# A two-block transformer kernel on one core: bias reads moved to SP's queue, GpSimd's work reordered and enlarged, convolution taps dealt anew

## The chip, the cores and the metric

The kernel runs on one core of one Trainium2 chip. The metric is the device time of one execution in microseconds. Engines are named as in the profile: PE (TensorE), DVE (VectorE), ACT (ScalarE), POOL (GpSimd), SP (SyncE, which here only issues transfers).

## The reference, cut to what matters

Two blocks run over one sequence of 256 tokens with 1024 channels, all in float32. Every large product is a projection `h @ W`.

```python
def first_block(x, ...):
    h = rms_norm(x, attn_norm_w)
    q, k, v, u, g = split(h @ w_in)                  # 1024 x (1024+1024+1024+2048+2048)
    q, k = rms_norm per head (8 heads, 2 x 64)
    p = softmax(q1 k1 * scale + bias) - lam * softmax(q2 k2 * scale + bias)   # bias from T5 buckets
    y_a = (rms_norm(p @ v) * c) @ w_proj_attn
    c = causal_depthwise_conv(u_a * sigmoid(u_b), width 31)
    y_b = silu(layer_norm(c)) @ w_proj_conv          # mean and variance over the channels
    x = x + (g_a * y_a + g_b * y_b) @ w_out
    return x + (silu(gt) * up) @ w_down              # feed-forward, 2816 wide

def second_block(x, ...):
    q, k, v, xl, gl = split(rms_norm(x) @ w_in_2)
    a = stick_breaking_attention(q, k, v)            # log-sigmoids and suffix sums
    l = rg_lru(conv4(xl)) * gelu(gl)                 # a linear recurrence over the tokens
    x = x + concat(a, l) @ w_out_2
    return x + square(relu(rms_norm(x) @ w_up)) @ w_down   # 4096 wide
```

## The kernel before

**Units.** All projections are cut into 120 units. A unit is a slab of weights of 4 x 128 rows by 512 columns (1 MB). For each unit SP issues the load into one of three `raw` slots; ACT rounds it to `w_hi` (`split_high`, L605); DVE or POOL subtracts to get the rest, `w_lo` (`split_low` L944, or L588 on POOL where `on_pool(u)` holds: units 7 to 27 without 18); PE then multiplies 4 x 2 x 3 times (L1691 to L1693: hi·hi, lo·hi, hi·lo). `w_hi` and `w_lo` have three slots too. Each engine has one program in a fixed order, a loop over the step `s`; in step `s` PE multiplies unit `s`, and ACT, DVE and POOL prepare unit `s + 2` and do the small work of that step. A load into a slot waits for the subtraction of the unit three before it (L427).

**Small work of PE.** It comes either in the middle of a unit (`halfway(s)`, after the second of four slabs) or behind it (`after(s)`). PE's small products go to four banks of `aux`; a bank is handed over by `claim`, which waits for the last reader.

**First mixer, steps 2 to 35.** The convolution is 248 taps on DVE (31 taps times 8 channel tiles of 128, L984 and L988), accumulated in `aux` bank 1, and dealt over the steps by a table:

```python
TAPS_AT = {3: 8, 4: 6, 5: 7, 6: 12, 7: 14, 8: 12, 9: 9, ..., 25: 10, 26: 12}
```

Steps 3 to 26 hold them all; `conv_last` is 26, and `LN` is 27. Taps of a pair of channel tiles need `glu_t` of that pair (`turn_glu(i)` on PE at L1504, kept by ACT at L671). A head's attention takes four steps from `HEADS[hd]` (8, 10, 12, 14, 18, 20, 22, 24): PE's scores; DVE adds the bias (L1130) and takes the maximum (L1136); ACT exponentiates; DVE makes the factor `st_mix` (L1109); POOL scales and adds the two maps (L556, L560) in step `HEADS[hd] + 2`; PE turns the result (`turn_probs`, after step `HEADS[hd] + 2`) and multiplies by v. POOL also sums conv tiles (L548, in the steps `ADDED`), scales attention outputs (L534 to L541, in the steps of `A_GROUPS`: 19, 26, 28) and raises to the power -1/2 (L484) for the norms of q and k.

**Bias.** `rel_row` is written to a scratch tensor in DRAM by POOL's queue (L514) and read back shifted by eight transfers of 128 KB, two in each of the steps 4 to 7, issued by POOL in `bias_reads` (L503 to L511). The first use is DVE's L1130 of head 0, in step 9.

**Channel norm.** When the last taps are done (step 26), DVE adds the last two conv tiles to `conv_sum` (L1220), PE makes the mean (`channel_sum(conv_sum, 0)`, halfway through step 27, in bank 2), DVE subtracts it (L1258), and squares, variance and gates follow.

**Second mixer, from step B = 74.** In the steps 80 to 85 DVE runs the recurrence (L1301 to L1313) and the softplus sums (`softplus_sum`, L1016 and L1020) which PE needs for `suffixes(n)` (L1442 to L1446): `suffixes(0)` halfway through unit 83, `suffixes(1)` behind it. ACT rounds units 83, 84 and 85 in the steps 81, 82 and 83; POOL does nothing there but the norm of q and k.

Of the kernel before, what the change touches and what calls it, by code (L numbers as in the profile page):

```python
# [14 lines left out]
P = 128  # L15
D = 1024
S = 256
# [66 lines left out]
def build(nc, a, out):  # L84
# [21 lines left out]
    PIECED = 3  # L106

# [10 lines left out]
    def on_pool(u):  # L118
        return 7 <= u <= 27 and u != 18
# [14 lines left out]
    TAPS_AT = {3: 8, 4: 6, 5: 7, 6: 12, 7: 14, 8: 12, 9: 9, 10: 15, 11: 10, 12: 12, 13: 7, 14: 12, 15: 11, 16: 4, 17: 11, 18: 16, 19: 8, 20: 12, 21: 11, 22: 12, 23: 10, 24: 12, 25: 10, 26: 12}  # L134
# [16 lines left out]
    with ExitStack() as ctx:  # L151
# [250 lines left out]
        def _(sp):  # L402
# [17 lines left out]
            for u, (c, k0, nk, _, _) in enumerate(units):  # L420
# [45 lines left out]
        def _(pool):  # L466
# [36 lines left out]
            def bias_reads(s):  # L503
                step = P // SHIFTS
                for r in range(2 * s - 8, 2 * s - 6) if 4 <= s <= step // 2 + 3 else ():
                    if r == 0:
                        pool.wait_ge(rel_stored, 16)
                    pool.wait_ge(unit_done, s)
                    src = bass.AP(tensor=rel_dram, offset=P - 1 - r,
                                  ap=[[RELS - step, SHIFTS], [RELS * SHIFTS, H], [1, S]])  # L510
                    pool.dma_start(bias[r:P:step, :, :], src).then_inc(bias_loaded, 16)  # L511

# [4 lines left out]
            for s in range(NU):  # L517
                if s < K0:
                    bias_reads(s)
                if s in ended:  # L520
# [3 lines left out]
                    if kind == "res" and i % 2 == 1 and i < 7:  # L524
                        st = stage_of(kind, i)
                        power(rstd[:, st, :], ms[:, st, :], mean_sq, st + 1, rstd_ready)
                        if st == 2:
                            qk_epsilon(2)
                for j, (at_, n0, n1) in enumerate(A_GROUPS):
# [20 lines left out]
                for hd in range(H):  # L550
                    if s == HEADS[hd] + 2:
                        pool.wait_ge(summed, 2 * hd + 2)
                        for qb in range(2):
                            n = 2 * hd + qb
                            p_1 = probs[:, 1, OFF[qb]:OFF[qb] + P * (qb + 1)]
                            nc.gpsimd.tensor_scalar(p_1, p_1, st_mix[:, n:n + 1], 0.0, ALU.mult, ALU.add)\  # L556
                                .then_inc(scaled, 1)
                        pool.wait_ge(scaled, 2 * hd + 2)
                        p_0, p_1 = probs[:, 0, 0:KEYS], probs[:, 1, 0:KEYS]
                        nc.gpsimd.tensor_tensor(p_0, p_0, p_1, ALU.add).then_inc(mixed, 1)  # L560
# [29 lines left out]
                if s >= K0:  # L590
                    bias_reads(s)
# [5 lines left out]
        def _(act):  # L597
# [109 lines left out]
            for s in range(NU + 1):  # L707
# [35 lines left out]
                if (0 < s < EARLY or s >= B) and s not in LATE and s not in (Q0, K0, LN + 2, LN + 3) and s not in NORMS and s + LEAD < NU:  # L743
# [172 lines left out]
                if s == B + 8:  # L916
                    softplus_parts(0)
                    split_high(s + LEAD)
                if s == B + 9:
                    keep_turned2(gelu_t, 0, g2_turned, g2_in)  # L920
                    softplus_parts(1)
                    split_high(s + LEAD)
                    act.wait_ge(lru_out, 1)
                    nc.scalar.activation(y_hi[:, CT2:KT, :], lru_tmp[:, :, :], ACT.Copy).then_inc(lru_hi, 1)
                    weights2(0)
# [14 lines left out]
        def _(dve):  # L940
# [124 lines left out]
            for s in range(NU + 1):  # L1065
# [691 lines left out]
```

## Time and profile before

| | |
|---|---|
| time, 3 runs | 737.78, 739.63, 741.29 us, median 739.63 |
| profiled execution | 738.59 us, of it 736.8 us from the first to the last instruction |
| PE busy | 726.5 us (99%), granted clock 1.00 |
| PE weight loads | 596.2 us (81%) |
| DVE, ACT, POOL busy | 486.3, 397.3, 167.9 us |
| HBM | 129.61 MB read, 178 GB/s over the span |

The profile is of one execution; times in it run from the first instruction. Busy PE time includes overlap of one product with the next, so the places to look at are those where PE stood idle before an instruction.

### The profile page before, as it was taken

How to read it: one execution, taken by the hardware profiler on the slowest of the kernel's cores; microseconds unless marked ns; L12 is line 12 of the kernel's file. 1: busy time of each engine (PE TensorE's matmuls, PEld its weight loads, DVE VectorE, ACT ScalarE, POOL GpSimd, SP SyncE). 2: the span in 40 equal slices, each digit the busy share in tenths (PEclk: the TensorE clock that was granted, in tenths of full speed). 3: DMA queues.
4: the chain of work that ended last, by engine and by line, in shares of the span. 5: the costliest groups of instructions: out<-in, count | busy, mean ns of one | idle time of the engine just before them, and what ended most of it. 6: DMA issues, size and time to landing. Idle time of an engine off the chain costs nothing.

```text
span 736.8 us, 9065 instructions
## 1 busy us (share of the span) xinstructions
PE 726.5 (99%) x3439; PEld 596.2 (81%) x3439; DVE 486.3 (66%) x659; ACT 397.3 (54%) x513; POOL 167.9 (23%) x118
## 2 busy tenths in 40 slices
PE   9998999999999999999999999999999999999998
PEld 7786778788788888888888888888788888888886
DVE  5598998999887665555556355668866565653531
ACT  6744667564794455444444345479846554444330
POOL 1089898998300011000000000140001000000000
PEclk9999999999999999999999999999999999999999
DMA  8866536555347546655664564642364556556540
GB/s 293 254 199 198 172 117 199 194 174 175 115 172 286 172 155 215 194 178 172 191 216 148 188 208 147 229 170 59 114 201 149 196 166 203 171 173 204 194 143 29
DMA packets 82851, 131.45 MB, mean 178 GB/s; under 512 B 4036, under 2 KB 35852, under 8 KB 82808
## 3 DMA queue, kind: packets, MB, share of 16 engines
q1 hardware_dynamic: 82272, 129.61, 53.8%
q0 software_dynamic: 528, 1.25, 0.6%
q8 instruction: 28, 0.46, 0.3%
q14 instruction: 15, 0.12, 0.0%
q10 hardware_dynamic: 8, 0.02, 0.0%
HBM read 129.61 MB, written 1.25 MB: 178 GB/s over the span
## 4 chain that ended last, share of the span: by engine, by line
PE 77%; DVE 9%; ACT 4%; POOL 4%; DMA 3%; issue 2%; SPq 0%; ACTq 0%; DVEq 0%; POOLq 0%
PE acc L1691 23%; PE acc L1693 23%; PE acc L1692 23%; PE aux L1351 4%; DVE aux L988 3%; POOL w_lo L588 3%; DMA raw<-w_in_dram 1%; ACT w_hi L605 1%; DVE w_lo L944 1%; DMA x_in<-x_dram 1%; DMA bias<-rel_scratch 1%; POOL probs L556 1%; DVE qk_ss L1151 0%; DVE w_lo L949 0%; PE aux L1397 0%
## 5 line engine op out<-in xcount | busy, mean ns | idle before, releaser
L944 DVE TENSOR_TENSOR w_lo<-raw,w_hi 128x2048 fp32r<-128x2048 f32 (+1 forms) x97 | 220.2, 2272 | 126.5 <-ACT w_hi L605 126.5
L605 ACT ACTIVATE w_hi<-raw 128x2048 fp32r<-128x2048 f32 (+1 forms) x117 | 221.9, 1900 | 137.9 <-PE acc L1693 132.8
L1691 PE MATMUL acc<-w_hi,h_hi 128*128 128x512 f32 x616 | 245.4, 398 | 0.6 <-POOL w_lo L588 0.3
L1693 PE MATMUL acc<-w_hi,h_lo 128*128 128x512 f32 x616 | 240.5, 390 | 0.0
L1692 PE MATMUL acc<-w_lo,h_hi 128*128 128x512 f32 x616 | 240.0, 390 | 0.0
L1691 PEld LDWEIGHTS acc<-w_hi,h_hi 128*128 128x128 f32 x616 | 115.8, 188 | 25.4 <-issue 2.0
L1693 PEld LDWEIGHTS acc<-w_hi,h_lo 128*128 128x128 f32 x616 | 115.6, 188 | 24.6
L1692 PEld LDWEIGHTS acc<-w_lo,h_hi 128*128 128x128 f32 x616 | 115.9, 188 | 22.6
L588 POOL TENSOR_TENSOR w_lo<-raw,w_hi 128x2048 fp32r<-128x2048 f32 x20 | 93.1, 4657 | 3.4 <-ACT w_hi L605 3.4
L988 DVE SCALAR_TENSOR_TENSOR aux<-glu_t,vec_t,aux 128x256 f32<-128x256 f32 x232 | 93.4, 481 | 0.0
L484 POOL TENSOR_TENSOR rstd<-ms,nhalf 128x2 f32<-128x2 f32 x4 | 8.7, 2183 | 333.4 <-DVE ms L971 333.4
L1691 PE MATMUL acc<-w_hi,m_hi 128*128 128x512 f32 x208 | 81.2, 390 | 0.0
L1693 PE MATMUL acc<-w_hi,m_lo 128*128 128x512 f32 x208 | 81.0, 389 | 0.0
L1692 PE MATMUL acc<-w_lo,m_hi 128*128 128x512 f32 x208 | 81.0, 389 | 0.0
L1691 PEld LDWEIGHTS acc<-w_hi,m_hi 128*128 128x128 f32 x208 | 39.0, 188 | 8.1
L1693 PEld LDWEIGHTS acc<-w_hi,m_lo 128*128 128x128 f32 x208 | 39.0, 188 | 8.1
L1692 PEld LDWEIGHTS acc<-w_lo,m_hi 128*128 128x128 f32 x208 | 39.0, 188 | 8.0
L632 ACT ACTIVATE m_hi<-aux 128x512 fp32r<-128x512 f32 x27 | 15.3, 597 | 54.6 <-PE aux L1351 54.6
L1691 PE MATMUL acc<-w_hi,y_hi 128*128 128x512 f32 x96 | 38.3, 399 | 0.6 <-DVE gates L1158 0.6
L1693 PE MATMUL acc<-w_hi,y_lo 128*128 128x512 f32 x96 | 37.5, 390 | 0.0
L1692 PE MATMUL acc<-w_lo,y_hi 128*128 128x512 f32 x96 | 37.4, 390 | 0.0
L963 DVE TENSOR_TENSOR m_lo<-aux,m_hi 128x512 fp32r<-128x512 f32 x27 | 17.9, 688 | 16.9 <-ACT m_hi L632 16.8
(229 smaller groups left out, 681.3 us busy)
## 6 DMA issues: line engine op xcount, KB each, us to landing
raw<-w_in_dram SPq DMA_DIRECT2D x29, 1024.0 KB, 5.2
raw<-w_down_dram SPq DMA_DIRECT2D x26, 1024.0 KB, 5.1
raw<-w_gate_up_dram SPq DMA_DIRECT2D x44, 512.0 KB, 4.6
raw<-w_up_dram SPq DMA_DIRECT2D x16, 1024.0 KB, 5.5
raw<-w_out_dram SPq DMA_DIRECT2D x8, 1024.0 KB, 5.5
raw<-w_in_dram SPq DMA_DIRECT2D x12, 512.0 KB, 4.7
raw<-w_proj_attn_dram SPq DMA_DIRECT2D x4, 1024.0 KB, 5.0
raw<-w_proj_conv_dram SPq DMA_DIRECT2D x4, 1024.0 KB, 5.0
```

What stands on the lines that cost most here:

```text
L484: nc.gpsimd.tensor_tensor(out_, in_, nhalf[:, 0:in_.shape[1]], ALU.pow).then_inc(s_out, 1)
L556: nc.gpsimd.tensor_scalar(p_1, p_1, st_mix[:, n:n + 1], 0.0, ALU.mult, ALU.add)\
L588: nc.gpsimd.tensor_tensor(w_lo[:, u % SPLIT, 0:nk, :], raw[:, u % RAW, 0:nk, :], f(w_hi[:, u % SPLIT, 0:nk, :]), ALU.subtract).then_inc(w_ ...
L605: nc.scalar.activation(w_hi[:, u % SPLIT, 0:nk, :], raw[:, u % RAW, 0:nk, :], ACT.Copy)\
L632: nc.scalar.activation(dst[:, 2 * g:2 * g + 2, :], aux[:, bank, :].rearrange("p (a b) -> p a b", a=2), ACT.Copy, scale=scale).then_inc(s_o ...
L944: nc.vector.tensor_tensor(w_lo[:, u % SPLIT, 0:nk, :], raw[:, u % RAW, 0:nk, :], f(w_hi[:, u % SPLIT, 0:nk, :]), ALU.subtract).then_inc(w_ ...
L963: nc.vector.tensor_tensor(lo[:, 2 * g:2 * g + 2, :], aux[:, bank, :].rearrange("p (a b) -> p a b", a=2), f(hi[:, 2 * g:2 * g + 2, :]), ALU ...
L988: nc.vector.scalar_tensor_tensor(out=conv_acc(ct) if tap < TAPS - 1 else conv[:, ct, :], in0=glu_t[:, ct, tap:tap + S], scalar=vcol(R_CONV ...
L1351: return nc.tensor.transpose(out_, in_, ident[:, :])
L1691: nc.tensor.matmul(o, x_h, w_hi[:, slot, j, :], start=begin_, stop=False)
L1692: nc.tensor.matmul(o, x_h, w_lo[:, slot, j, :], start=False, stop=False)
L1693: mm = nc.tensor.matmul(o, x_l, w_hi[:, slot, j, :], start=False, stop=end_)
```

## The change

It has these parts. (1) The eight bias reads go from POOL's queue to SP's: two behind each of the loads of units 7 to 10, with a wait for the scratch tensor ahead of the first. (2) On POOL the mixing of a head (L556, L560) comes ahead of the scaling of attention outputs and of the conv sums in the same step. (3) `on_pool` takes unit 28 as well. (4) POOL rounds units 83 and 84 (`split_high` on POOL, one `tensor_scalar` each); ACT's roundings of them go away, and ACT's rounding of unit 85 comes behind `y_hi`. (5) On DVE, in step 82 the subtraction of unit 84 comes ahead of `softplus_sum(0)`, and in step 83 `log_weights(0)` behind `y_lo`. (6) The channel sum goes to bank 1 and behind unit 26, and DVE's centring to the head of step 27. (7) `turn_glu(0)` goes from the middle of unit 3 to behind it. (8) The taps are dealt anew; step 16 may run two taps early; two and no longer four go ahead of `norm_qk` of q1. With the new table a pair of tiles ends at 62 taps in step 8 (before: 59 there), and `ADDED` goes from 10, 15, 21 to 9, 16, 22; `conv_last` stays 26, with 5 taps for 7.

```diff
+    READS = 7
...
-        return 7 <= u <= 27 and u != 18
+        return 7 <= u <= 28 and u != 18
...
-    TAPS_AT = {3: 8, 4: 6, 5: 7, 6: 12, 7: 14, 8: 12, 9: 9, 10: 15, 11: 10, 12: 12, 13: 7, 14: 12, 15: 11, 16: 4, 17: 11, 18: 16, 19: 8, 20: 12, 21: 11, 22: 12, 23: 10, 24: 12, 25: 10, 26: 12}
+    TAPS_AT = {3: 8, 4: 6, 5: 4, 6: 13, 7: 14, 8: 17, 9: 9, 10: 14, 11: 9, 12: 11, 13: 7, 14: 10, 15: 13, 16: 7, 17: 11, 18: 16, 19: 8, 20: 8, 21: 12, 22: 13, 23: 10, 24: 12, 25: 11, 26: 12}
...
+                if READS <= u < READS + 4:
+                    if u == READS:
+                        sp.wait_ge(rel_stored, 16)
+                    step = P // SHIFTS
+                    for r in (2 * (u - READS), 2 * (u - READS) + 1):
+                        src = bass.AP(tensor=rel_dram, offset=P - 1 - r,
+                                      ap=[[RELS - step, SHIFTS], [RELS * SHIFTS, H], [1, S]])
+                        sp.dma_start(bias[r:P:step, :, :], src).then_inc(bias_loaded, 16)
...
+            def split_high(u):
+                nk = units[u][2]
+                pool.wait_ge(w_hi_ready, u)
+                pool.wait_ge(raw_in[u % RAW], raw_value[u])
+                pool.wait_ge(unit_done, u - SPLIT + 1)
+                nc.gpsimd.tensor_scalar(w_hi[:, u % SPLIT, 0:nk, :], raw[:, u % RAW, 0:nk, :], 1.0, 0.0, ALU.mult, ALU.add)\
+                    .then_inc(w_hi_ready, 1)
...
+                if s in (B + 7, B + 8):
+                    split_high(s + LEAD)
...
-                if s == B + 8:
-                    softplus_parts(0)
-                    split_high(s + LEAD)
...
+                if s == LN:
+                    dve.wait_ge(ln_sum, 1)
+                    for hf in range(2):
+                        ch = conv[:, 4 * hf:4 * hf + 4, :]
+                        nc.vector.tensor_tensor(ch, ch, again(aux[:, CONV_BANK, 0:S], 4), ALU.subtract).then_inc(ln_centered, 1)
...
-                early = 0 if s in avail.values() or s in (Q0, Q0 + 1, K0, K0 + 1, K1, K1 + 1) else min(quota[s], 2)
+                early = 0 if s in avail.values() or s in (Q0, Q0 + 1, K0, K0 + 1, K1 + 1) else min(quota[s], 2)
...
-                        ahead = 0 if (kind, i) != ("q", 1) else min(4, quota[s] - early)
+                        ahead = 0 if (kind, i) != ("q", 1) else min(2, quota[s] - early)
...
+                    split_low(s + LEAD)
                     softplus_sum(0)
-                    split_low(s + LEAD)
...
-                for i in range(4):
+                for i in range(1, 4):
                     if s == end["u", i] + 1:
                         turn_glu(i)
...
+                if s == end["u", 0] + 1:
+                    turn_glu(0)
...
+                if s == conv_last:
+                    pe.wait_ge(sum_added, 2)
+                    channel_sum(conv_sum[:, :], 0)
```

## Rows read from the trace of the kernel before

**Rows 1.** PE's timeline where it stood idle (start, us, what, [idle before, releaser]).
```profile
31.24 0.44 PE L1351 MATMUL aux<-ident,glu 128*128 128x128 f32 x2 [0.45 <-DVE glu L1007]
...
58.00 0.47 PE L1691 MATMUL acc<-w_hi,h_hi 128*128 128x512 f32 x1 [0.31 <-POOL w_lo L588]
...
70.22 0.52 PE L1351 MATMUL aux<-ident,glu 128*128 128x128 f32 x3 [1.80 <-DVE probs L1130]
...
99.80 0.50 PE L1691 MATMUL acc<-w_hi,h_hi 128*128 128x512 f32 x1 [0.30 <-DVE tok L999]
...
186.02 0.55 PE L1351 MATMUL aux<-ident,probs 128*128 128x128 f32 x3 [1.16 <-POOL probs L560]
...
200.09 0.50 PE L1691 MATMUL acc<-w_hi,y_hi 128*128 128x512 f32 x1 [0.62 <-DVE gates L1158]
...
512.34 0.70 PE L1442 MATMUL aux<-w_t,neg_tri 128*128 128x256 f32 x2 [0.24 <-DVE w_t L1020]
...
517.57 0.70 PE L1442 MATMUL aux<-w_t,neg_tri 128*128 128x256 f32 x2 [0.42 <-DVE w_t L1020]
```
**Rows 2.** DVE's timeline, 48 to 70 us.
```profile
48.20 1.27 DVE L1151 TENSOR_REDUCE qk_ss<-qk_square 128x8 f32<-128x512 f32 x2
...
62.34 4.00 DVE L988 SCALAR_TENSOR_TENSOR aux<-glu_t,vec_t,aux 128x256 f32<-128x256 f32 x10
69.05 1.02 DVE L1130 SCALAR_TENSOR_TENSOR probs<-aux,bias 128x256 f32<-128x256 f32 x2 [2.71 <-DMA bias<-rel_scratch]
```
**Rows 3.** POOL's timeline, stretches from 43 to 496 us.
```profile
43.52 1.12 POOL L511 DMA_DIRECT2D bias<-rel_scratch  x2
...
53.20 4.66 POOL L588 TENSOR_TENSOR w_lo<-raw,w_hi 128x2048 fp32r<-128x2048 f32 x1
...
97.84 4.64 POOL L588 TENSOR_TENSOR w_lo<-raw,w_hi 128x2048 fp32r<-128x2048 f32 x1
...
182.02 2.87 POOL L556 TENSOR_SCALAR probs<-probs,st_mix 128x128 f32<-128x128 f32 x2
184.97 0.99 POOL L560 TENSOR_TENSOR probs<-probs 128x384 f32<-128x384 f32 x1
...
493.18 2.90 POOL L484 TENSOR_TENSOR qk_r<-qk_ss,nhalf 128x16 f32<-128x16 f32 x1
```
**Rows 4.** DMA issues by line (count, KB each, median us to landing).
```profile
bias<-rel_scratch POOLq DMA_DIRECT2D x8, 128.0 KB, 3.9
```
**Rows 5.** DVE's timeline, 100 to 200 us.
```profile
100.25 2.26 DVE L1109 SCALAR_TENSOR_TENSOR st_mix<-st_rec,small,st_sum 128x2 f32<-128x2 f32 x1
...
166.62 0.22 DVE L1109 SCALAR_TENSOR_TENSOR st_mix<-st_rec,small,st_sum 128x2 f32<-128x2 f32 x1
...
178.74 0.73 DVE L1109 SCALAR_TENSOR_TENSOR st_mix<-st_rec,small,st_sum 128x2 f32<-128x2 f32 x1
...
181.50 2.69 DVE L944 TENSOR_TENSOR w_lo<-raw,w_hi 128x2048 fp32r<-128x2048 f32 x1
...
186.07 0.94 DVE L1220 TENSOR_TENSOR conv_sum<-conv_sum,conv 128x256 f32<-128x256 f32 x2
...
198.63 1.40 DVE L1158 SCALAR_TENSOR_TENSOR gates<-acc,rstd,gate_bias 128x512 f32<-128x512 f32 x2
```
**Rows 6.** Groups of POOL's instructions by form (count, busy us, mean ns, idle before).
```profile
L556 POOL TENSOR_SCALAR probs<-probs,st_mix 128x256 f32<-128x256 f32 x8 | 3.8, 480 | 0.0
```
**Rows 7.** The instructions of line L556 (ns: least, median, most).
```profile
L556 POOL TENSOR_SCALAR probs<-probs,st_mix x16: 369/476/2409, 75.3 to 184.4; 128x128 f32<-128x128 f32 x8, 128x256 f32<-128x256 f32 x8
```
**Rows 8.** DVE's timeline in the second mixer, 497 to 511 us.
```profile
497.32 1.22 DVE L1301 TENSOR_TENSOR in_gate<-in_gate,lru_u 128x1024 f32<-128x1024 f32 x1
498.70 1.23 DVE L1303 TENSOR_TENSOR decay_gate<-decay 128x1024 f32<-128x1024 f32 x1 [0.17 <-ACT decay L911]
...
504.08 1.22 DVE L1310 TENSOR_TENSOR in_gate<-in_gate,lru_tmp 128x1024 f32<-128x1024 f32 x1 [0.69 <-issue]
...
510.34 0.96 DVE L1016 SCALAR_TENSOR_TENSOR w_t<-aux,soft 128x768 f32<-128x768 f32 x1 [2.56 <-ACT soft L687]
```

More of the change, by code:

```diff
@@ L501, in _ @@
             qk_epsilon(0)
[L503 to L511, printed above, removed]
             pool.wait_ge(rel_kept, 1)
@@ L517, in _ @@
             for s in range(NU):
-                if s < K0:
-                    bias_reads(s)
                 if s in ended:
@@ L528, in _ @@
                             qk_epsilon(2)
+                for hd in range(H):
+                    if s == HEADS[hd] + 2:
+                        pool.wait_ge(summed, 2 * hd + 2)
+                        for qb in range(2):
+                            n = 2 * hd + qb
+                            p_1 = probs[:, 1, OFF[qb]:OFF[qb] + P * (qb + 1)]
+                            nc.gpsimd.tensor_scalar(p_1, p_1, st_mix[:, n:n + 1], 0.0, ALU.mult, ALU.add)\
+                                .then_inc(scaled, 1)
+                        pool.wait_ge(scaled, 2 * hd + 2)
+                        p_0, p_1 = probs[:, 0, 0:KEYS], probs[:, 1, 0:KEYS]
+                        nc.gpsimd.tensor_tensor(p_0, p_0, p_1, ALU.add).then_inc(mixed, 1)
                 for j, (at_, n0, n1) in enumerate(A_GROUPS):
@@ L549, in _ @@
                                                     conv[:, ct, :], ALU.add).then_inc(conv_added, 1)
[L550 to L560, printed above, removed]
                 if s == begin["ff", 3]:
@@ L589, in _ @@
                                             f(w_hi[:, u % SPLIT, 0:nk, :]), ALU.subtract).then_inc(w_lo_pool, 1)
-                if s >= K0:
-                    bias_reads(s)
                 if s in ended and s != K0 and ended[s][0] in ("q", "k") and ended[s][1] < 2:
@@ L742, in _ @@
                             keep_qk(kind, i, 1)
-                if (0 < s < EARLY or s >= B) and s not in LATE and s not in (Q0, K0, LN + 2, LN + 3) and s not in NORMS and s + LEAD < NU:
+                if (0 < s < EARLY or s >= B) and s not in LATE and s not in (Q0, K0, LN + 2, LN + 3, B + 7) and s not in NORMS and s + LEAD < NU:
                     split_high(s + LEAD)
@@ L921, in _ @@
                     softplus_parts(1)
-                    split_high(s + LEAD)
                     act.wait_ge(lru_out, 1)
                     nc.scalar.activation(y_hi[:, CT2:KT, :], lru_tmp[:, :, :], ACT.Copy).then_inc(lru_hi, 1)
+                    act.wait_ge(w_hi_ready, s + LEAD)
+                    split_high(s + LEAD)
                     weights2(0)
@@ L1254, in _ @@
                 if s == LN:
-                    dve.wait_ge(ln_sum, 1)
-                    for hf in range(2):
-                        ch = conv[:, 4 * hf:4 * hf + 4, :]
-                        nc.vector.tensor_tensor(ch, ch, again(aux[:, 2, 0:S], 4), ALU.subtract).then_inc(ln_centered, 1)
                     split_low(s + LEAD)
@@ L1321, in _ @@
                     softplus_sum(1)
-                    log_weights(0)
                     dve.wait_ge(lru_hi, 1)
@@ L1325, in _ @@
                         .then_inc(lru_lo, 1)
+                    log_weights(0)
                     log_weights(1)
@@ L1419, in channel_sum @@
             def channel_sum(src, n):
-                claim([2], *((ln_centered, 2) if n == 0 else (ln_var, 1)))
-                nc.tensor.matmul(aux[:, 2, 0:S], mean_w[:, :], src, start=True, stop=True).then_inc(ln_sum, 1)
+                bank = (CONV_BANK, 2)[n]
+                claim([bank], *((ln_centered, 2) if n == 0 else (ln_var, 1)))
+                nc.tensor.matmul(aux[:, bank, 0:S], mean_w[:, :], src, start=True, stop=True).then_inc(ln_sum, 1)
             def scores2(n):
@@ L1514, in halfway @@
                         attend(hd)
-                if s == LN:
-                    pe.wait_ge(sum_added, 2)
-                    channel_sum(conv_sum[:, :], 0)
                 if s in a_steps:
```

## The prediction, written before the change was run

> **What bounds the kernel now.** I read the busy times first: PE is busy for 726.5 of 736.8 us, at a granted clock of 1.00 throughout, and the change takes no product off it. So the change can only give back time in which PE stood idle, and the next view is PE's own timeline at each such place [rows 1]. Those are eight waits: 0.45, 0.31, 1.80, 0.30, 1.16, 0.62, 0.24 and 0.42 us, 5.30 us in all. That sum, 0.7% of the time, is the most that the change can give, whatever it takes off the other engines. DVE, ACT, POOL and SP matter only through what they hand to PE at these places, and through new places that they open. A measurement of this kernel can tell about 0.5%, 3.7 us, from no change, so the whole question is whether two thirds or more of the 5.30 us come back.
>
> I then followed each wait one engine further, in DVE's and POOL's timelines, since the cause of a wait is in the order of their programs.
>
> **The glu turn in unit 3 (0.45).** PE waits for DVE's product in the middle of the unit. Behind the unit, some 2.7 us later, the product is long there, and the taps that need its result start at 35.28, later than the turned tile is kept even then. Worth 0.45; at worst 0, if the later turn delays the first tap.
>
> **The bias reads (0.31 and 1.80).** PE's 1.80 at 70.22 is behind DVE's bias add, and that one waited 2.71 us for the last bias read [rows 2]. On POOL the reads stand behind subtractions of 4.66 us, and cost POOL 0.55 each [rows 3]. On SP the last pair is issued with unit 10's load, which waits for unit 7's subtraction on POOL, near 49; with 3.9 us to land [rows 4] it is there more than 10 us before its use. So DVE's wait for it goes. But the new table puts taps in its place. Up to DVE's add at step 9 the plan holds 62 taps and no longer 59, and DVE is busy without a gap from 48.20 to 66.34, so its add moves by three taps of 0.39 us (ten in 4.00 [rows 2]): 62.34 + 4.00 + 1.2 = 67.5. From that add to PE's turn it was 70.22 - 69.05 = 1.17, so PE goes on at 68.7 and no longer at 70.22. That is 1.5 us, and it holds the 0.45 and whatever part of the 0.31 comes back: some 1.0 us of waiting stays here. I take 1.55 for the three places together. The bounds: 0, were the reads still late; 2.56, were nothing left to wait for. SP's new wait at unit 7 holds the loads of unit 8 and later: it delays unit 8's load from 35.4 to some 38.4, since POOL's own first read of the scratch could start only at 37.4. The load takes about 5 us, and ACT rounds unit 8 at 46.8, so 3 us of cover are left; without that cover the delay would come out at PE in full.
>
> **norm_qk of q1 (0.30).** PE waits 0.30 for DVE's tile, with four taps ahead of it. Two fewer give DVE 0.8 us; then POOL's power is the last to end, about 0.7 us ahead of the old start. Worth 0.25 (0 to 0.30).
>
> **Steps 26 to 28 (1.16 and 0.62).** The mix of the last head ended at 185.96 because POOL scaled two attention tiles first and because its scaling then took 2.87 us [rows 3] for what in a free stretch takes 0.37 + 0.48 [rows 6, 7]. That second part is a collision: DVE's subtraction of 181.50 runs over the same time and is itself 0.4 us longer than elsewhere [rows 5]. The same shows from the other side: the tiny L1109 takes 0.22 alone, but 2.26 at 100.25, until POOL's subtraction of 97.84 ends, and 0.73 at 178.74 [rows 3, 5]. So an instruction of DVE with two inputs from SBUF and one of POOL exclude each other for their whole length, and the one that waits goes next. The Trainium skill's page "SBUF — State Buffer" (Who interferes with whom) says the same and draws the line: a DVE instruction with at most one input from SBUF does not contend, which the taps at 0.39 us beside POOL's subtractions bear out.
>
> With the mix first, it starts at st_mix and is done 2.0 us later, near 182 on the old scale, and PE needs it at 184.7: the 1.16 goes. Against it, the channel sum now stands right behind. It needs DVE's two sums. DVE no longer subtracts unit 28 (2.69 [rows 5]), so they move from 187.0 to 184.3, plus two more taps dealt ahead of step 26 and fewer in it (0), plus collisions with POOL (0.5 for one attention tile; up to 0.7 at st_mix of head 6, as POOL's conv sums now stand behind the mix of step 22 and push a subtraction of 4.66 onto it): 185.2. PE gets there at 185.1. I put 0.2 us of new wait here, and 0.95 for the term (0 to 1.16). Behind it, DVE centres some 3 us sooner, before its attention tile, its subtraction of unit 29 waits for POOL's of unit 28 (4.66, done 2 us before PE needs it), and the gates, which ended at 200.03 [rows 5], come out about 3.7 us sooner while PE is about 2.8 sooner: the 0.62 goes. I take 0.6 (0 to 0.62).
>
> These terms make 1.55 + 0.25 + 0.95 + 0.6 = 3.35 us saved before the feed-forward.
>
> **Second mixer (0.24 and 0.42).** Two things are added to DVE's path to the first softplus sum. First, the subtraction of unit 84 now comes ahead of it: 2.25 us. Second, POOL's two roundings collide with DVE, which here runs nothing but instructions with two SBUF inputs. The trace has no rounding on POOL. From `tensor_scalar` of 128 and of 256 elements, 369 and 480 ns [rows 6, 7], the slope is 0.87 ns an element, so 2048 take about 2.0 us; from above it is bounded by the subtraction's 4.65, which reads two tensors; from below by nothing under the 1.9 us that ACT takes. I take 2.0, as it is the same operation. POOL is free at 493.18 + 2.90 = 496.1 [rows 3] and rounds unit 83 until 498.1; DVE's L1301 of 497.32 [rows 8] waits 0.7. The rounding of unit 84 may start when unit 81 is multiplied, near 501.25, while DVE is in its chain; it goes next when DVE's running instruction ends and costs DVE its whole 2.0. Together 2.25 + 0.7 + 2.0 = 4.95. DVE had idle time on this path of 0.17 + 0.69 + 2.56 = 3.42 [rows 8]; the last of these was a wait for ACT, which now, without its rounding, comes sooner. So the sum is 1.5 us later, and PE's wait of 0.24 grows by 1.2 to 1.5. The next one, 0.42, goes, as PE arrives later and ACT and DVE have less ahead of the second sum. Net: a loss of 0.9 us. Without the collision the path has 3.42 - 2.25 = 1.2 us to spare, and both waits go: a gain of 0.66. That is the upper bound. The lower is the dear rounding, below. The roundings leave ACT 3.8 us freer, which is hidden, since ACT ends no wait of PE here except through DVE.
>
> Everything behind unit 86 is untouched.
>
> **The sum.** 3.35 - 0.9 = 2.45 us saved. The profiled execution took 738.59 us (736.8 of it span), so 736.1 (span 734.3). The median of the runs shown is 1.04 above the profiled one, which gives 737.1 us, 0.3% less.
>
> **Rivals.**
> (a) *No collision in the second mixer:* POOL's roundings fall into DVE's gaps, or do not exclude it. For it: ACT's and DVE's times there may shift by the microsecond that decides; against: DVE has no gap of 2 us before the sum at which unit 84 may be rounded. It gives 3.35 + 0.66 = 4.0, 735.6 us, faster by 0.54%.
> (b) *All eight waits go:* DVE gains in steps 5 to 8 more than the three taps cost, for instance because POOL's subtraction of unit 8 (53.20 [rows 3]) comes earlier. 5.3 us, 734.3.
> (c) *POOL's subtraction of unit 28 gets in between DVE's two sums:* the second then waits its 4.66, and PE with it, near 3.7 after what is won. By my count the second sum is asked for 0.8 us before that subtraction could begin, both counted from st_mix. It gives 3.9 us more than my sum, 737.1 + 3.9 = 741.0, 0.2% above the median before, no measurable change. From more than 0.8 us of delay on DVE's side it decides.
> (d) *The rounding on POOL is dear,* the slower case. At 4.65 each, L1301 waits 3.4, the second costs 4.65, and with 2.25 the path is 10.3 - 3.4 = 6.9 us late, from 1.2 us on visible at PE. 737.1 + 5.4 = 742.5, and 743 with unit 83's own subtraction late: slower by 0.4 to 0.5%. Against it: the slope of [rows 6, 7] is that of the same operation.
> (e) *The change does not do what it says for the reads:* SP's wait at unit 7 lasts longer, and unit 8 comes late. It costs PE what it is beyond 3 us.
>
> **How the numbers follow.** My forecast's own case (between 1 and 3.7 us saved) gets 0.48; (a) 0.25; (b) 0.08; (c) 0.08; (d) 0.06; (e) and the rest 0.05. Faster by over 0.5% (below 735.9) are (a) and (b) and the edge of the forecast, less the edge of (a): 0.34. Slower by over 0.5% are most of (d) and half of (e): 0.06. The rest, 0.60, is the same. The range takes in all of (a), most of (b) and the upper part of the forecast's case up to (c): 734.3 to 740.3. The forecast's own range is 735.9 to 738.7.
>
> **What the profile after would show.** No idle time of PE before the turn at 31; about 1.0 us before the one near 69; none before the mix turn near 183 and 0 to 0.5 before the channel sum behind it; none at unit 29; 1.2 to 1.8 us at the first suffix product near 510. POOL's rounding at about 2.0 us, the second or a DVE neighbour stretched by that much. DVE's L1130 of head 0 without a wait for a transfer. PE's busy time as before. The prediction is wrong if the suffix product waits less than 0.3 us (then it is (a)), or if a wait of over 1 us stands at a place that [rows 1] does not name.

## The result, and the profile after

| | before | after |
|---|---|---|
| median (lowest to highest), runs | 739.06 us (737.78 to 741.29), 4 | 733.89 us (733.45 to 734.54), 4 |
| ratio to before, 95% interval | | 0.9927 (0.9909 to 0.9945) |
| profiled execution, its span | 738.59, 736.8 us | 734.1, 732.3 us |
| PE busy; POOL busy | 726.5; 167.9 us | 724.5; 172.2 us |

The change saves 5.2 us, 0.7%, where 2.5 was forecast (737.1 us). It came out 0.4 us below the low end of the range, and faster by more than 0.5%, which had 34%.

PE's waits after, grouped by who ended them (total, times, longest; the 1.6 for `ident` is at the start and stood there before too):

```profile
engine line waited for: us in total, times, longest us
PE aux L1357 <- POOL ident L478: 1.6, 1, 1.6
PE aux L1449 <- DVE w_t L1025: 1.0, 1, 1.0
PE aux L1357 <- DVE probs L1140: 0.7, 1, 0.7
PE aux L1357 <- DVE y_lo L1049: 0.4, 1, 0.4
PE acc L1700 <- DVE tok L1004: 0.4, 1, 0.4
```

Of the eight waits of [rows 1], those for the glu turn in unit 3, POOL's `w_lo`, norm_qk of q1 (0.30), the mix of the last head (1.16) and the gates (0.62) are gone. The 1.80 before the turn near 70 is 0.7. A new 0.4 stands in step 27 before the turn of an attention tile (`y_lo`, at 186.56; at the channel sum itself, at 182.10, PE does not wait), and another 0.4 at norm_qk of q0. The second mixer has one wait of 1.0 in place of 0.24 and 0.42. So of the 5.30 us of idle time 2.8 are gone.

DVE's timeline after, in step 8, and PE's of its turn behind that (start, duration, instruction, and in brackets the idle time before it and who ended it):

```profile
60.77 5.20 DVE L993 SCALAR_TENSOR_TENSOR aux<-glu_t,vec_t,aux 128x256 f32<-128x256 f32 x13
65.86 0.89 DVE L993 SCALAR_TENSOR_TENSOR conv<-glu_t,vec_t,aux 128x256 f32<-128x256 f32 x2
66.64 1.04 DVE L1140 SCALAR_TENSOR_TENSOR probs<-aux,bias 128x256 f32<-128x256 f32 x2
```

```profile
67.83 0.63 PE L1357 MATMUL aux<-ident,glu 128*128 128x128 f32 x4 [0.72 <-DVE probs L1140]
```

DVE runs taps without a gap up to its bias add, and the add no longer waits for a transfer, against 2.71 us before [rows 2]. What PE waits for here is now DVE's own queue. SP's queue after:

```profile
36.57 1.25 SPq L445 DMA_DIRECT2D bias<-rel_scratch  x2
37.92 0.54 SPq L433 DMA_DIRECT2D raw<-w_in_dram  x1
38.50 1.18 SPq L445 DMA_DIRECT2D bias<-rel_scratch  x2
```

Unit 8's load is issued at 37.92, 2.5 us later than before (35.44), or 3.2 once the 0.74 us are taken out by which this execution was ahead from its start (below). No wait of PE comes of it. The last pair of reads is issued at 48.6, as counted.

The second mixer after, DVE and then POOL over the same stretch:

```profile
496.83 2.28 DVE L949 TENSOR_TENSOR w_lo<-raw,w_hi 128x2048 fp32r<-128x2048 f32 x1
499.03 2.92 DVE L1316 TENSOR_TENSOR in_gate<-in_gate,lru_tmp 128x1024 f32<-128x1024 f32 x1
501.99 2.44 DVE L1319 TENSOR_TENSOR_SCAN lru_u<-decay,in_gate 128x256 f32<-128x256 f32 x4
504.34 2.27 DVE L949 TENSOR_TENSOR w_lo<-raw,w_hi 128x2048 fp32r<-128x2048 f32 x1
506.52 0.95 DVE L1021 SCALAR_TENSOR_TENSOR w_t<-aux,soft 128x768 f32<-128x768 f32 x1
```

```profile
491.53 1.92 POOL L495 TENSOR_SCALAR w_hi<-raw 128x2048 fp32r<-128x2048 f32 x1
496.82 4.06 POOL L495 TENSOR_SCALAR w_hi<-raw 128x2048 fp32r<-128x2048 f32 x1 [3.38 <-PE acc L1702]
```

POOL's first rounding takes 1.92 us, where 2.0 was estimated. The second begins with DVE's subtraction of unit 83; the subtraction keeps its 2.28, the rounding takes 4.06, and L1316 behind it takes 2.92 and not the 1.22 of before: all three end as if POOL's 1.9 us had been set between the two of DVE, for 1.7 us of DVE's path. DVE's L1021 has no wait for ACT ahead of it any more (2.56 in [rows 8]). The row to look for in such a case is not POOL's but its neighbour's.

**Where the 4.5 us between the two profiles arose.** The difference of the times at which a unit's last product began, before less after:

| behind unit | 0 | 3 | 6 | 8 | 9 | 14 | 27 | 29 | 83 | 84 |
|---|---|---|---|---|---|---|---|---|---|---|
| us | 0.74 | 1.87 | 0.79 | 1.31 | 2.42 | 2.93 | 3.65 | 4.55 | 3.82 | 4.53 |

The 0.74 is there before anything of the change has acted. Without it: 1.7 up to unit 9, 0.5 for q1, 1.6 in steps 26 to 28, and nothing in the second mixer (0.7 lost behind unit 83, 0.7 back behind 84); 3.8 in all. The 1.87 behind unit 3 is not all a gain: the glu turn, which before lay inside the unit, now comes after its last product. Behind unit 4 the difference is 1.37, and the new wait at q0 brings it down to 0.79 behind unit 6.

**Why 3.8 and not 2.8.** The idle time that went is 2.8 us, and PE is busy 2.0 us less (724.5 for 726.5), though no product was taken off it; 1.0 of this lies behind unit 2, the rest in the start. The rows show why. Products begin 0.23 us apart and are shown 0.39 long, so in dense work they overlap, and ahead of a wait they do not. PE at the start of unit 29, before (with the wait for the gates) and after (without):

```profile
198.88 0.59 PE L1421 MATMUL aux<-centered_sq,mean_w 128*128 128x256 f32 x2
200.09 0.50 PE L1691 MATMUL acc<-w_hi,y_hi 128*128 128x512 f32 x1 [0.62 <-DVE gates L1158]
```

```profile
195.23 0.59 PE L1428 MATMUL aux<-centered_sq,mean_w 128*128 128x256 f32 x2
195.47 0.58 PE L1700 MATMUL acc<-w_hi,y_hi 128*128 128x512 f32 x1
```

From start to start it is 1.21 us before and 0.24 after: a wait listed as 0.62 took 0.97, and the whole unit is 0.90 shorter. A listed wait of PE is thus less than what it costs: by 0.3 us here, and by 0.2 at norm_qk of q1 (0.5 for 0.30).

### The profile page after: what moved, and what is told of

Read it like the earlier page. It is cut to its first block, busy times and chain, and to the rows that moved or that the text cites. A ratio compares the mean times of both kernels' runs of the same rounds, so it can differ in the third digit from the quotient of the medians.

```text
span 732.3 us, 9064 instructions
## 1 busy us (share of the span) xinstructions
PE 724.5 (99%) x3439; PEld 596.0 (81%) x3439; DVE 485.8 (66%) x658; ACT 394.2 (54%) x511; POOL 172.2 (24%) x113
## 4 chain that ended last, share of the span: by engine, by line
PE 85%; DVE 8%; DMA 2%; ACT 2%; issue 1%; POOL 1%; SPq 1%; DVEq 0%; ACTq 0%
PE acc L1700 26%; PE acc L1702 26%; PE acc L1701 26%; PE aux L1357 4%; DVE aux L993 3%; DMA raw<-w_in_dram 2%; DVE w_lo L949 1%; ACT w_hi L610 1%; PE aux L1403 1%; PE aux L1421 1%; PE aux L1449 1%; DVE tok L1004 1%; DVE qk_ss L1161 0%; POOL qk_r L501 0%; DVE in_gate L1316 0%
## 5 line engine op out<-in xcount | busy, mean ns | idle before, releaser
L949 DVE TENSOR_TENSOR w_lo<-raw,w_hi 128x2048 fp32r<-128x2048 f32 x96 | 217.6, 2269 | 126.5 <-ACT w_hi L610 126.5
L610 ACT ACTIVATE w_hi<-raw 128x2048 fp32r<-128x2048 f32 (+1 forms) x115 | 218.1, 1901 | 137.2 <-PE acc L1702 134.2
L595 POOL TENSOR_TENSOR w_lo<-raw,w_hi 128x2048 fp32r<-128x2048 f32 x21 | 98.7, 4708 | 1.5 <-ACT w_hi L610 1.4
```

Source lines behind the costliest of these rows:

```text
L595: nc.gpsimd.tensor_tensor(w_lo[:, u % SPLIT, 0:nk, :], raw[:, u % RAW, 0:nk, :], f(w_hi[:, u % SPLIT, 0:nk, :]), ALU.subtract).then_inc(w_ ...
L610: nc.scalar.activation(w_hi[:, u % SPLIT, 0:nk, :], raw[:, u % RAW, 0:nk, :], ACT.Copy)\
L949: nc.vector.tensor_tensor(w_lo[:, u % SPLIT, 0:nk, :], raw[:, u % RAW, 0:nk, :], f(w_hi[:, u % SPLIT, 0:nk, :]), ALU.subtract).then_inc(w_ ...
```

## The experiments

There were three sets of runs, each on one chip, with the kernel before run again on it: 739.65 us (737.78 to 742.63, 17 runs) beside the first four below, 740.02 (737.46 to 742.11, 23) beside the next three and the last, 739.77 (736.18 to 741.29, 11) beside the four between them. Ratios are to these, with 95% intervals. "Change" is the kernel after.

**The change again**, without an edit.

> The changed kernel once more, to see its level and its first 15 us again. In the first pair of profiles the changed kernel was already 0.74 us ahead at the end of unit 0, before any part of the change acts. Theory A (that is chance: the moment from which PE's products run at their short spacing differs from run to run): unit 0 ends anywhere between 14.3 and 15.2 us in this profile, and 4.5 to 5.2 us are saved in the times. Theory B (the change itself shortens the start): unit 0 ends at 14.4 again here and in every kernel built on the changed one, and at 15.1 in those built on the one before.

733.82 us (733.33 to 735.07, 6 runs), 0.9915 (0.9899 to 0.9932). The last product of unit 0 began at 14.34; in the two first profiles it was 15.15 before and 14.40 after. Over the fourteen profiles of this case, whose programs are alike up to there, it lies anywhere from 13.7 to 15.4 (below). So the 0.74 is chance.

**The change with the second mixer's edits undone.**

> The changed kernel with everything in the second mixer put back: units 83 and 84 rounded by ACT, the softplus sum ahead of the subtraction of unit 84, log_weights(0) ahead of y_lo. My forecast's reading (the second mixer's edits lose 0.9 us): 0.9 us faster than the changed kernel. The reading of its trace (they lose 0.72 at the first suffix product and win 0.71 at the second): the same within 0.2 us. Rival (a) of the forecast (they win 0.66): 0.7 us slower than the changed kernel.

```diff
-                if s in (B + 7, B + 8):
-                    split_high(s + LEAD)
...
-                    split_low(s + LEAD)
                     softplus_sum(0)
+                    split_low(s + LEAD)
```

(and ACT's roundings of units 83 to 85 and `log_weights(0)` where they were). 734.42 us (733.72 to 734.8, 6), 0.9921 (0.9905 to 0.9937). Unit 84's last product begins at 521.93, in the repeated change at 521.96. The second mixer's edits give nothing and cost nothing that shows; the forecast was a loss of 0.9.

**The kernel before with the second mixer's edits alone.**

> The kernel before with the second mixer's edits alone. Forecast: 0.9 us slower than before, PE's wait at the first suffix product 1.4 us. Reading of the trace after: within 0.2 us of before, with about 0.96 us of wait at the first suffix product and none at the second; the second rounding on POOL shows 4.1 us or its neighbour on DVE is stretched by 1.7. Rival (a): 0.7 us faster.

The reverse of the diff above, on the kernel before. 740.65 us (738.44 to 742.2, 12), 1.0012 (0.9998 to 1.0026). By the times alone this is no measurable change, but it could hide the 0.9 us of the forecast. The profile decides it: against the kernel before, this one is 3.61 us behind at unit 82, 4.29 at unit 83 and 3.58 at unit 84, so the edits lose 0.7 and give it back, as in the change. But its profiled execution took 742.2 us, 3.6 more than the one on which the prediction rests, and not because of these edits. DVE's and PE's timelines:

```profile
70.93 1.02 DVE L1140 SCALAR_TENSOR_TENSOR probs<-aux,bias 128x256 f32<-128x256 f32 x2 [3.93 <-DMA bias<-rel_scratch]
```

```profile
72.10 0.63 PE L1361 MATMUL aux<-ident,glu 128*128 128x128 f32 x4 [2.98 <-DVE probs L1140]
```

And its windows of four microseconds (busy time and instructions of each engine, then the granted clock, the DMA share and the GB/s):

```profile
core 0: us, PE busy (x) PEld busy (x) DVE busy (x) ACT busy (x) POOL busy (x), PEclk, DMA share, GB/s
72.00:76.00 4.00, 3.90 (x14) 3.24 (x15) 3.89 (x10) 3.21 (x9) 3.11 (x2) 0.68 0.74 229
76.00:80.00 4.00, 4.00 (x17) 3.19 (x16) 3.96 (x13) 3.47 (x7) 2.69 (x4) 0.90 0.68 250
```

The wait for the last bias read is 3.93 us here and not 2.71 [rows 2], PE's is 2.98 and not 1.80 [rows 1], and when PE goes on, its granted clock is 0.68 for four microseconds and 0.90 for the next four. The missing parts, 0.32 x 4 and 0.10 x 4, make 1.7 us, which is 3.4 us at 0.50: for 3.4 us PE ran at the lower of its two levels, 1.2 and not 2.4 GHz. The Trainium skill ("TensorE: Matmul & The Clock Gate", The HAM clock gate) says the same of the levels: full or half, nothing between; a mean of 0.68 is a mix in time.

**The change with `softplus_sum(0)` ahead of the subtraction again.**

> The changed kernel with one edit undone: in step 82 softplus_sum(0) comes ahead of the subtraction of unit 84 again, while POOL keeps its two roundings. If the order is what makes PE's 0.96 us of wait at the first suffix product: that wait is gone (the subtraction's 2.27 us lie behind it) and the kernel is 1.0 us faster than the changed one. If the collision of POOL's roundings with DVE (1.7 + 0.5 us) is enough by itself: the wait stays at 0.5 us or more.

```diff
+                    softplus_sum(0)
                     split_low(s + LEAD)
-                    softplus_sum(0)
```

732.95 us (731.52 to 733.85, 6), 0.9903 (0.9883 to 0.9922). The suffix wait is gone, 0.9 us better than the change. That order was the part of the change that hurt. Against the kernel before, this version gains 1.2 us between units 82 and 84, where waits of 0.24 and 0.42 went.

**The kernel before with the bias reads on SP alone.**

> The kernel before with the bias reads on SP's queue and nothing else. Theory C (the wait for the last bias read is not 1.8 us of PE's time but a length that differs from execution to execution, 1.8 us in the profile of before and 3.0 in that of the last experiment, and from some length on it costs the granted clock as well, 0.5 for 3.4 us there; that is why the kernel before spreads from 737.8 to 742.6 and the changed one only from 733.3 to 735.1): this part alone saves 2.5 to 4 us in the medians, its runs lie within 2 us of each other, DVE's add no longer waits for a transfer, and the granted clock is 1.00 throughout. Theory D (the wait is worth what the profile of before shows, 1.80, and the spread of before has another source): 1.8 us saved, and the runs still spread over 4 us.

```diff
+    READS = 7
+                if READS <= u < READS + 4:
+                    if u == READS:
+                        sp.wait_ge(rel_stored, 16)
...
+                        sp.dma_start(bias[r:P:step, :, :], src).then_inc(bias_loaded, 16)
-                if s < K0:
-                    bias_reads(s)
-                if s >= K0:
-                    bias_reads(s)
```

736.08 us (735.25 to 736.45, 5), 0.9951 (0.9934 to 0.9967). This one part gives 3.9 us of the change's 5.8 (739.65 less 733.82), and the spread over the runs falls from 4.7 us to 1.2. In its profile DVE's add starts at 65.55 with no wait, and PE does not wait at the turn.

**The change with the reads back on POOL.**

> The changed kernel with the bias reads put back on POOL's queue. Theory C: the wait and the spread are back, 2 to 4 us slower than the changed kernel, over a spread of 3 us or more; DVE's add waits for a transfer. Theory D: 1.0 us slower (DVE's add comes 1.1 us after where the taps would let it), no wider spread.

The reverse diff, on the change. 738.18 us (735.24 to 739.01, 12), 0.9973 (0.9959 to 0.9986). All else that the change does is worth 1.8 us. In its profiled execution DVE's add waited 2.55 us for the reads. PE's timeline and the window behind it:

```profile
70.65 0.63 PE L1363 MATMUL aux<-ident,glu 128*128 128x128 f32 x4 [2.88 <-DVE probs L1146]
```

```profile
72.00:76.00 4.00, 4.00 (x12) 3.11 (x11) 3.96 (x13) 3.47 (x11) 1.78 (x1) 0.57 0.51 135
```

Again the clock is down behind the wait: PE ran 12 instructions in four microseconds.

**The kernel before with the reads on SP, but with the loads of units 9 to 12.**

> The kernel before with the bias reads on SP's queue, but two behind each of the loads of units 9 to 12 and no longer 7 to 10, so that the last pair is issued near 64, as in the kernel before. If the time of issue is what matters: DVE's add still waits for a transfer, 2 us or more, and the time is within 1 us of before. If the kind of queue is what matters (a transfer issued by POOL lands late or unevenly): no wait, and the time of the reads-only kernel.

```diff
+    READS = 9
```

(the rest as in the diff of the reads alone). 739.47 us (737.0 to 740.88, 12), 0.9990 (0.9977 to 1.0004): as the kernel before. SP's queue, DVE, PE and the window behind the wait:

```profile
62.88 1.19 SPq L445 DMA_DIRECT2D bias<-rel_scratch  x2
```

```profile
69.05 1.02 DVE L1125 SCALAR_TENSOR_TENSOR probs<-aux,bias 128x256 f32<-128x256 f32 x2 [3.31 <-DMA bias<-rel_scratch]
```

```profile
70.22 0.63 PE L1346 MATMUL aux<-ident,glu 128*128 128x128 f32 x4 [2.42 <-DVE probs L1125]
```

```profile
72.00:76.00 4.00, 4.00 (x13) 3.18 (x12) 3.86 (x13) 3.47 (x11) 1.40 (x3) 0.62 0.81 265
```

The last pair is issued at 62.88, on POOL's queue before it was 63.55, and with the early reads 48.62. So what counts is when the reads are issued, not which engine's queue holds them, nor the time that POOL spent on issuing.

**The kernel before once more.**

> The kernel before, unchanged, for a second profile of it. Theory C (the wait at the glu turn near 70 us differs from execution to execution and takes the clock with it from some length on): the wait differs from 1.80 us, or the clock falls to 0.5 for 3.41 us behind it, or both, and time minus 735 grows with it. Theory D: 1.8 us again, clock 1.00.

739.46 us, one run. DVE, PE and the window behind the wait:

```profile
69.84 1.02 DVE L1130 SCALAR_TENSOR_TENSOR probs<-aux,bias 128x256 f32<-128x256 f32 x2 [3.76 <-DMA bias<-rel_scratch]
```

```profile
71.01 0.63 PE L1351 MATMUL aux<-ident,glu 128*128 128x128 f32 x4 [2.82 <-DVE probs L1130]
```

```profile
72.00:76.00 4.00, 4.00 (x19) 3.30 (x18) 3.86 (x13) 3.97 (x12) 2.24 (x2) 1.00 0.68 195
```

PE's wait is 2.82 us, 1.0 longer than in the profile of the prediction, in the same program; its wait in unit 3 is 1.0 and not 0.45. Here the clock stayed at 1.00, and PE ran 19 instructions in the window. So the length of the wait alone does not decide whether the clock falls: 2.82 left it up here, 2.42 brought it down above. What the clock costs can be read from unit 9, from the last product of unit 8 to its own: 10.02 us here, and 11.18 in the kernel with the late reads on SP, where the wait was 0.4 shorter and the clock was down, so about 1.6 us.

**Taps dealt as before, in the change.**

> The changed kernel with the taps dealt as before (table, early taps in step 16, four ahead of norm_qk of q1). By the forecast the three more taps ahead of DVE's bias add cost PE 0.7 us at the glu turn: that wait is gone. Against it, 0.3 us come back at norm_qk of q1, 0.3 at unit 8, and two taps more lie ahead of the last sums, 0.8 us at the channel sum behind unit 26. Together 0 to 1 us slower than the changed kernel. Rival (the dealing is what makes the rest of the change pay): 2 us slower or more.

```diff
-    TAPS_AT = {3: 8, 4: 6, 5: 4, 6: 13, 7: 14, 8: 17, 9: 9, ..., 25: 11, 26: 12}
+    TAPS_AT = {3: 8, 4: 6, 5: 7, 6: 12, 7: 14, 8: 12, 9: 9, ..., 25: 10, 26: 12}
```

(and the two limits for taps ahead of the small work). 733.54 us (732.86 to 733.86, 6), 0.9919 (0.9897 to 0.9941). The wait at the turn near 68 goes, as three fewer taps stand ahead of the add, and 0.3 for POOL's `w_lo` and 0.3 at norm_qk of q1 come back; at norm_qk of q0 there is no wait. The new dealing is worth nothing: this is 0.3 us below the change, within the spread.

**The mixing behind the other work of POOL, in the change.**

> The changed kernel with POOL's mixing of a head behind the scaling of attention outputs and the conv sums again. The forecast put 1.16 us on this order: PE's wait for POOL at the turn behind unit 26 is back. DVE no longer subtracts there, so POOL's scaling takes 0.83 and not 2.87 us, and the mix ends 2.0 us sooner than in the kernel before: no wait at the turn, less than 0.5 us slower than the changed kernel. If the order by itself is what counts: 1.0 us slower or more.

The two hunks that move the mixing are undone. 733.78 us (733.05 to 734.59, 6), 0.9922 (0.9902 to 0.9943): as the change. POOL in step 26, first in the change and then in this kernel:

```profile
177.22 0.83 POOL L540 TENSOR_SCALAR probs<-probs,st_mix 128x128 f32<-128x128 f32 x2 [0.66 <-DVE st_mix L1119]
178.13 1.01 POOL L544 TENSOR_TENSOR probs<-probs 128x384 f32<-128x384 f32 x1
```

```profile
177.76 1.19 POOL L546 TENSOR_TENSOR a_tok<-a_tok,a_r 128x256 f32<-128x256 f32 x2
178.92 0.83 POOL L561 TENSOR_SCALAR probs<-probs,st_mix 128x128 f32<-128x128 f32 x2
179.84 1.28 POOL L565 TENSOR_TENSOR probs<-probs 128x384 f32<-128x384 f32 x1
```

In the old order the scaling takes 0.83 and not the 2.87 of [rows 3], since DVE has no subtraction of unit 28 there, and the mix is done at 181.1, ahead of PE's turn at 181.6. Without the collision the old order costs nothing.

**Unit 28 on DVE and the channel sum in unit 27, in the change.**

> The changed kernel with unit 28 subtracted by DVE and the channel sum in the middle of unit 27, bank 2, again. The forecast put 0.6 us on them at unit 29: the wait for the gates is back, and the kernel is 0.6 us slower than the changed one, up to 0.9; the mix stays ahead, so that there is no wait at the turn behind unit 26. Rival: DVE's subtraction (2.3 us) was hidden all along, no difference.

```diff
-        return 7 <= u <= 28 and u != 18
+        return 7 <= u <= 27 and u != 18
-                if s == conv_last:
+                if s == LN:
                     pe.wait_ge(sum_added, 2)
                     channel_sum(conv_sum[:, :], 0)
```

(the `LN` form in the middle of the unit, with bank 2 and the centring behind as before). 734.35 us (733.4 to 735.01, 6), 0.9929 (0.9909 to 0.9950), 0.5 above the change, with overlapping ranges; the wait of 0.6 for the gates is back (which of the two edits brings it, this run does not part), and the 0.4 behind `y_lo` is gone. The mix is done at 179.55 here, and the turn behind it waits for nothing: with the mix first, the collision costs PE nothing either. The 1.16 took both, the old order and DVE's subtraction. The collision of POOL and DVE is back too, only on a smaller victim (POOL's and DVE's timelines):

```profile
179.50 2.39 POOL L550 TENSOR_TENSOR a_ms<-a_ss,a_e 128x4 f32<-128x4 f32 x1
```

```profile
179.55 2.28 DVE L949 TENSOR_TENSOR w_lo<-raw,w_hi 128x2048 fp32r<-128x2048 f32 x1
```

An instruction on four elements, 0.20 us in the change at the same place, takes 2.39, until DVE's subtraction is over. With the mix ahead of it, it is this one that waits, and nobody waits for it.

**The waits that were left.**

> The changed kernel with softplus_sum(0) ahead of the subtraction of unit 84 and three smaller edits, each at a wait that the profile after still shows: DVE makes y_lo of the first two attention tiles ahead of the centring (0.43 us of PE's wait), 5 and 5 taps for 6 and 4 in steps 4 and 5 (0.2 to 0.4 us at norm_qk of q0), 15 and 11 for 17 and 9 in steps 8 and 9 (0.72 us at the glu turn). If the waits are independent: 0.9 + 0.43 + 0.3 + 0.72 = 2.3 us faster than the changed kernel, 731.5. If what is taken off at the glu turn comes back in the steps behind it, 1.5 us.

```diff
-    TAPS_AT = {3: 8, 4: 6, 5: 4, 6: 13, 7: 14, 8: 17, 9: 9, ...
+    TAPS_AT = {3: 8, 4: 5, 5: 5, 6: 13, 7: 14, 8: 15, 9: 11, ...
+                for at_, pairs in a_steps.items():
+                    if s == at_ + 1 and at_ != LN + 2:
+                        for g in pairs:
+                            a_low(g)
                 if s == LN:
                     dve.wait_ge(ln_sum, 1)
...
+                    softplus_sum(0)
                     split_low(s + LEAD)
-                    softplus_sum(0)
```

732.25 us (731.59 to 732.76, 4), 0.9899 (0.9881 to 0.9918): the fastest version, 1.6 us below the change. Beside the 1.6 for `ident` and 0.2 for `x_res`, which every version has, PE waits once:

```profile
PE acc L1700 <- DVE tok L1004: 0.4, 1, 0.4
```

Net of this wait, 4.95 of the 5.30 us of [rows 1] are gone here, and with the start taken out unit 84 comes 6.4 us sooner than before (7.0 less 0.6).

**The start and the clock, over all runs.** Unit 0's last product began, in microseconds: before 15.15, after 14.40, and in the order of the experiments above 14.34, 14.60, 15.42, 14.37, 14.37, 14.73, 14.63, 14.38, 13.73, 13.78, 13.74, 14.54. Nothing that was edited acts before it. The mean granted clock of an execution splits the runs of the kernel before (51 in the three sets) in two:

| kernel | mean clock 1.000: runs, median | 0.999 | below: runs, median |
|---|---|---|---|
| before | 21, 738.49 us | 0 | 30, 740.44 us (0.995 or 0.998) |
| reads back | 3, 735.98 | 0 | 9, 738.32 |
| reads late on SP | 4, 737.23 | 0 | 8, 740.03 |
| second mixer alone | 2, 739.15 | 0 | 10, 741.08 |
| the change (both sets) and the seven other versions with early reads | 47, 733.82 | 2 | 0 |

Each kernel with late reads has both kinds, 1.9 to 2.8 us apart; of 49 runs with early reads none is of the second kind (the two at 0.999 took 733.45 and 734.64 us). That the clock fell behind this wait is seen in three profiled executions; for the other runs only the mean is known. Between the executions with a mean of 1.000 the reads alone are worth 2.4 us (738.49 less 736.08).

## Why the prediction was wrong

The step that failed is the one on the bias reads. The prediction took the 1.80 us of one execution for the size of the wait, and carried the 1.04 us between that execution and the median over to the changed kernel. The runs show a wait of 1.8 to 3.0 us, often with a fall of the clock behind it, and the reads alone are worth 3.9 us in the medians.

The result lies 3.2 us below the forecast: 1.2 by the step from the profiled time to the median, 0.9 by the second mixer, 0.7 by chance at the start of the two profiles, and 0.4 by small differences in the other terms.

**The bias reads, and the step from the profiled time to the median.** The term "1.55 for the three places together" was near for the execution that it was read from: 2.42 - 0.74 up to unit 9 make 1.7, and PE goes on at 67.83, which with the 0.74 is 68.6, where 68.7 was said. In part that is luck: the idle time gone at these places is 1.4, since the 0.4 at q0 was not foreseen, and the rest is overlap (below). But the wait of 1.80 was one draw. In other executions with the reads as late as before it was 2.42, 2.82, 2.88 and 2.98, and in 30 of 51 runs of the kernel before the mean clock was below 1. The reads alone are worth 3.9 us in medians, more than twice the term and above its upper bound of 2.56 (though the interval of the ratio, 2.4 to 4.9 us, just takes that bound in). "The median of the runs shown is 1.04 above the profiled one" was the sign of this, and it was carried over as a constant: but the gap goes with the executions in which the clock fell. Those of the kernel before at a mean clock of 1.000 have a median of 738.49, at the 738.59 of the profiled one; it was of the favourable kind, and with the change all of them are. After the change, the median is 0.2 below the profiled time. This step is 1.2 us of the miss. It shifted the other bounds too: 5.30 us, "the most that the change can give", is no bound when the same waits are longer in the next execution.

**Idle time is less than a wait costs.** The 5.30 us are no bound for a second reason. The terms before the feed-forward, 3.35, were for the most part added up from idle times. The idle time gone there is 3.1, less than forecast, and the gain is 3.8; the version with four more edits gains 6.4 us with 4.95 of idle time gone. The overlap of products that a wait interrupts makes the difference. "PE's busy time as before" failed by this, 1.0 us of it behind unit 2.

**The second mixer, "a loss of 0.9 us".** Measured: 0.0 between the profiles, 0.6 gained (change against the version without these edits, within the spread) and between 0.2 gained and 1.9 lost (edits alone, by the interval), with 0.0 in that profile too. The price of a rounding was right (1.92), and so was the place of both: the first, behind the power of `qk_r`, stretched the recurrence's first multiplication (L1301, now L1307) from 1.22 to 1.72, and the second the one at L1316 by 1.7. Only the sizes were off: 0.5 for 0.7 and 1.7 for 2.0, since more of each lay beside an instruction that DVE was running anyway. With the 2.25 for the subtraction that is 4.45 against 3.42 of idle time, so 1.0 later, of which the wait of PE, 0.96 for 0.24, shows 0.72; and the 0.42 behind it went, as said. The loss by waits is 0.3 and not 0.9, and at the end of unit 84 not even that, as one wait interrupts the products once where two did it twice. The step of the change that did harm was named rightly: with the sum ahead of the subtraction again, 0.9 us came back.

**The rest of the profiled difference** is the start (0.74, chance) and q1 (0.5, forecast 0.25).

**What was right.** The steps 26 to 28: 1.6 for a forecast of 1.55, but partly by luck. The forecast had 0.2 of new wait at the channel sum (0 to 0.5); there is none there, and 0.43 stands 4.5 us later, behind `y_lo`, which the centring now precedes (it is gone in the version with `y_lo` ahead of the centring and in the one with the centring in its old place). The idle time gone is 1.35, and overlap gave the rest. Both causes given for the mix's 1.16, POOL's order and the collision, hold, and it took the two together: to undo either is enough. SP's wait at unit 7 delayed unit 8's load by 2.5 to 3.2 us (forecast 3.0) and was covered. The suffix wait, 1.0, is below the 1.2 to 1.8 announced.

**The rivals.** (a) gave 735.6 us for no collision; the collision is there. (b), all waits gone, 734.3 us, came nearest in time, but four of PE's waits remained; its number was met by chance, through longer waits before and the overlap, not through fewer waits after. (c) did not come: POOL's subtraction of unit 28 starts at 181.91, 0.4 us after DVE's two sums, which took 1.17 us from 180.31. (d) fell with the 1.92. (e) fell with the load of unit 8, covered. Of my own rivals in the experiments, a worth of the new dealing of taps and of the mixing's order fell too.

**Open.** What makes the last read land later in one execution than in another, no run here tells; it is not the time of issue (in the second profile of the kernel before, the last pair was issued 0.3 us sooner, at 63.28, and the wait ended 0.8 later). Nor is it shown why the clock fell behind a wait of 2.42 us and not behind one of 2.82. The new 0.4 at norm_qk of q0 was not followed up: it was anything from none to 1.6 in the profiles of kernels with the new table there. With the old table, or with 5 and 5 taps in steps 4 and 5, the profiles show none, which points at the taps.

## What to carry to other kernels

A wait that a transfer ends is a sample, not a size: before it goes into a sum, look at the spread of the times, and when the profiled run is faster than the median, ask whether the wait under study makes the difference. If it does, the change takes the spread away too, and the gap to the median must not be carried over. Where VectorE and GpSimd collide, look at the neighbour's duration, not only at waits, and there are two ways out: to move the large two-input instruction to the other engine, or to put what TensorE needs ahead of the collision; here either was enough. And the idle time listed for TensorE was less than the wait cost: compare the starts of products with and without it.

## What the runs showed of the hardware

- A wait of PE of 2.4 to 3.0 us was followed, in some executions and not in others, by about 3.4 us at a granted clock of 0.50. It costs 1.7 us in the windows, on top of the wait. The medians of executions with and without it are 1.9 to 2.8 us apart, which may hold longer waits as well.
- Eight reads of 128 KB out of DRAM, issued beside loads of 1 MB, took 3.9 to 4.3 us to land on POOL's queue and 5.4 to 5.8 on SP's (medians in one execution each). SP's queue was not quicker; it was only earlier.
- POOL's rounding of 2048 elements a partition (one input) took 1.92 us alone and 4.06 when it was asked for with a two-input subtraction on DVE. DVE's subtraction kept its length, and DVE's next instruction then waited for POOL's. The Trainium skill ("SBUF — State Buffer", Who interferes with whom) describes the lock, held for a whole instruction, and these rows agree. They show further that the two engines take turns when both have work queued.
- Products of PE of 128x512 begin 0.23 us apart and are shown 0.39 long. A wait listed as 0.62 us of idle time lengthened the time from start to start by 0.97, and one unit by 0.90.
